# Two-block transformer kernel: choice of experts on VectorE in another order and layout, and products with both parts of x joined into one

## The reference

```python
def squared_relu_mlp(h, w_up, w_down):          # w_up 1024 x 4096, w_down 4096 x 1024
    return jnp.square(jax.nn.relu(h @ w_up)) @ w_down
```

```python
q = (t @ w_q).reshape(T, 8, 2, 128)
s = jnp.einsum('thsd,hskd->thsk', q, sub_keys)          # 2 x 128 scores per head
v_half, i_half = lax.top_k(s, 16)
cand = (v_half[:, :, 0, :, None] + v_half[:, :, 1, None, :]).reshape(T, 8, 256)
best, pos = lax.top_k(cand, 16)
i1 = take_along_axis(i_half[:, :, 0], pos // 16); i2 = take_along_axis(i_half[:, :, 1], pos % 16)
experts, gates = i1 * 128 + i2, softmax(best)
act = gelu(einsum('td,tkd->tk', x, expert_u[experts])) * gates
out = einsum('tk,tkd->td', act, expert_v[experts])
```

## Time and profile before

| | us |
|---|---|
| median of 3 runs (lowest, highest) | 1515.65 (1515.44, 1515.95) |
| the profiled execution | 1515.26 |
| its span | 1513.5 |
| PE busy | 1435.5 (95%) |
| DVE busy | 1060.0 (70%) |
| ACT busy | 757.6 (50%) |
| POOL busy | 70.2 (5%) |

### The profile page before, as it was taken

How to read it: one execution, slowest core, us unless ns; L and a number is a source line. 1 busy time by engine, 2 the same in 40 slices (tenths; PEclk the granted TensorE clock), 3 DMA queues, 4 the chain that set the end, 5 groups by cost and what they waited for, 6 DMA issues and landing times.

```text
span 1513.5 us, 26922 instructions
## 1 busy us (share of the span) xinstructions
PE 1435.5 (95%) x9273; PEld 1293.6 (85%) x9273; DVE 1060.0 (70%) x1981; ACT 757.6 (50%) x1211; POOL 70.2 (5%) x87
## 2 busy tenths in 40 slices
PE   7889889999899997989989999999999999999997
PEld 7867769899798886889979999999999999988886
DVE  6897665555668577569997999555555555567775
ACT  6644654444556533454544555444444444444453
POOL 0200100000000621000000000000000000000000
PEclk9999999999999999999999999999999999999999
DMA  7442325565344522454546888755757566577753
GB/s 280 139 130 96 126 84 188 186 192 183 112 144 161 169 82 70 153 181 154 167 152 185 256 257 259 226 189 184 249 183 245 182 220 210 190 239 249 249 194 140
DMA packets 103208, 274.54 MB, mean 181 GB/s; under 512 B 8160, under 2 KB 41056, under 8 KB 102640
## 3 DMA queue, kind: packets, MB, share of 16 engines
q1 hardware_dynamic: 64832, 237.11, 48.4%
q10 hardware_dynamic: 38032, 34.63, 6.8%
q0 software_dynamic: 288, 2.10, 0.4%
HBM read 254.93 MB, written 18.87 MB: 181 GB/s over the span
## 4 chain that ended last, share of the span: by engine, by line
PE 80%; DVE 15%; ACT 2%; issue 2%; POOL 0%; DMA 0%; POOLq 0%; ACTq 0%; DVEq 0%; SPq 0%
PE Y L1803 43%; PE AO L1803 34%; DVE wl L950 4%; DVE CV L1034 2%; PE M L1803 2%; ACT wh L471 1%; DVE eqs L1558 1%; DVE I L1478 1%; DVE SCO L1494 1%; DVE I L1492 1%; DVE PU L1533 0%; DVE V L1500 0%; DVE V L1486 0%; DVE eqs L1572 0%; DVE xn L973 0%
## 5 line engine op out<-in xcount | busy, mean ns | idle before, releaser
L950 DVE TENSOR_TENSOR wl<-raw,wh 128x1024 fp32r<-128x1024 f32 x440 | 541.6, 1234 | 278.2 <-ACT wh L471 277.4
L471 ACT CAST wh<-raw 128x1024 fp32r<-128x1024 f32 x440 | 460.0, 1048 | 186.7 <-PE AO L1803 92.3
L1803 PE MATMUL AO<-xh,wh 128*128 128x256 f32 (+1 forms) x1776 | 511.0, 288 | 8.6 <-DVE wl L950 7.3
L1803 PE MATMUL AO<-xh,wl 128*128 128x256 f32 (+1 forms) x1776 | 503.4, 283 | 0.0
L1803 PE MATMUL AO<-xl,wh 128*128 128x256 f32 (+1 forms) x1776 | 503.4, 283 | 0.0
L1803 PEld LDWEIGHTS AO<-xh,wh 128*128 128x128 f32 x1776 | 338.5, 191 | 16.3 <-DVE wl L950 9.0
L1803 PEld LDWEIGHTS AO<-xl,wh 128*128 128x128 f32 x1776 | 337.8, 190 | 4.6 <-issue 0.2
L1803 PEld LDWEIGHTS AO<-xh,wl 128*128 128x128 f32 x1776 | 338.7, 191 | 0.0
L1803 PE MATMUL Y<-wh,peer_ah 128*128 128x512 f32 x512 | 200.7, 392 | 2.1 <-DVE peer_al L1620 2.1
L1803 PE MATMUL Y<-wh,peer_al 128*128 128x512 f32 x512 | 200.3, 391 | 0.0
L1803 PE MATMUL Y<-wl,peer_ah 128*128 128x512 f32 x512 | 199.1, 389 | 0.0
(11 more groups left out here) (305 smaller groups left out, 1672.2 us busy)
## 6 DMA issues: line engine op xcount, KB each, us to landing
raw<-in_stream SPq DMA_DIRECT2D x440, 512.0 KB, 3.4
gate_spill<-gstage ACTq DMA_DIRECT2D x32, 512.0 KB, 5.2
gates<-gate_spill ACTq DMA_DIRECT2D x6, 2048.0 KB, 14.9
gates<-gate_spill ACTq DMA_DIRECT2D x8, 512.0 KB, 7.2
rowg<-in_post SPq DMA_DIRECT2D x3, 512.0 KB, 4.4
X<-in_x SPq DMA_DIRECT2D x2, 512.0 KB, 4.8
memx<-in_mem SPq DMA_DIRECT2D x1, 1024.0 KB, 8.1
keys<-in_keys POOLq DMA_DIRECT2D x1, 1024.0 KB, 6.7
```

The lines of the kernel that those rows point to most:

```text
L471: nc.scalar.copy(wh[:, s, :], raw[:, s, :]).then_inc(split_hi, 1)
L950: nc.vector.tensor_tensor(wl[:, s, :], raw[:, s, :], wh[:, s, :].bitcast(F32), ALU.subtract)\
L1803: return nc.tensor.matmul(o, a, b, start=start, stop=stop)
```

## The change

In the MLP and in the paired stage, x's two parts lie side by side in one tile, and the high weights meet both in one matmul of 512 columns that fills a whole bank of AO; the low weights times `xh` go into the first half. The halves are then added: ACT copies the second, DVE adds the first. In the paired stage DVE's sum goes to `up_s` and ACT does the gelu from there, one chunk later.

In the choice of experts the estimates of `turn` are others, the sum keeps its remainder, the layouts put heads innermost, the table of ranks holds each rank 128 times (17 x 128, made by POOL later), PE turns NAT round after chunk 26 (FIRST_TURN), and the last two plain chunks come behind it. ACT's plain chunks 20 to 28 are written out.

```diff
+FIRST_TURN = PLAIN - 2
+SPLIT_EVERY = 1.55
...
-        xh = sb("xh", [P, KT, TM], F32R)
-        xl = sb("xl", [P, KT, TM], F32R)
+        xhl = sb("xhl", [P, KT, 2, TM], F32R)
+        xh, xl = xhl[:, :, 0, :], xhl[:, :, 1, :]
...
ACT, mlp
-                    nc.scalar.activation(hid[:, s, :], AO[:, s, 0:T], func).then_inc(a_free, 1)
+                    nc.scalar.copy(hid[:, s, :], AO[:, s, T:]).then_inc(hid_part, 1)
ACT, plain chunks
+            for c in range(EXP_AT, PLAIN):
+                if c == FIRST_TURN:
+                    act.wait_ge(top_turn, 1)
+                    for j in range(TT):
+                        nc.scalar.copy(picks[:, :, P * j:P * j + P],
+                                       M[:, j, 0:3 * P].rearrange("p (n t) -> p n t", n=3)).then_inc(top_T, 1)
+                hidden(c, P0 + c, c)
+                split(P0 + 4, c)
ACT, both
-                act.wait_ge(hid_lo, c + (FF_CHUNKS + 1))
                 split(P0 + AHEAD + 4 + 2 * s, 0, i)
-                nc.scalar.activation(hid[:, c, :], AO[:, s, 0:T], ACT.Gelu).then_inc(a_free, 1)
+                if not (type(c) is int and c == 0):
+                    act.wait_ge(a_free, c + (A_BASE["peer"] + AHEAD))
+                nc.scalar.copy(up_l[:, s, :], AO[:, s, T:]).then_inc(up_part, 1)
+                if not (type(c) is int and c == 0):
+                    curved(c - 1, 1 - s)
+            def curved(c, s):
+                nc.scalar.activation(hid[:, c, :], up_s[:, s, :], ACT.Gelu).then_inc(curve, 1)
...
+            act.wait_ge(a_free, A_BASE["peer"] + AHEAD + PAIRED)
+            curved(PAIRED - 1, 1)
DVE, mlp (and low now stands ahead of the first split)
+                    dve.wait_ge(hid_part, i * 2 + (base + s + 1))
+                    nc.vector.tensor_tensor(hid[:, s, :], AO[:, s, 0:T], hid[:, s, :], ALU.add).then_inc(a_free, 1)
                     dve.wait_ge(a_free, i * 2 + (free_base + s + 1))
DVE, turn
-                if turns[0] > 1.5 and turns[1] < PLAIN:
+                while turns[0] >= SPLIT_EVERY and turns[1] < FIRST_TURN:
                     split(P0 + 4, turns[1])
-                    turns[0] = 0.0
+                    turns[0] -= SPLIT_EVERY
                     turns[1] += 1
DVE, choice (estimates of max 0.13 to 0.14, index and replace 0.21 to 0.27, shifts 0.2 and 0.33 to 0.29 and 0.45)
-            turn(nc.vector.tensor_copy(I16B[:, :, :, :], I16[:, :, :, :]), 0.6)
+            for j in range(TT):
+                turn(nc.vector.tensor_copy(I16B[:, j, :, :, :].rearrange("p s a h -> p h s a"),
+                                           I16[:, j, :, :].rearrange("p (h s) a -> p h s a", s=2)), 0.35)
...
-                                                 PF[:, half, j, :][:, :, None].to_broadcast([P, HK, TOPK]),
-                                                 ranks[:, half, :][:, None, :].to_broadcast([P, HK, TOPK]),
-                                                 ALU.is_equal), 1.1)
+                                                 PF[:, half, j, :][:, None, :].to_broadcast([P, TOPK, HK]),
+                                                 ranks[:, 1 - half:TOPK + 1 - half, :], ALU.is_equal), 1.25)
...
-                        e, e, IB[:, j, :, half, :][:, :, None, :].to_broadcast([P, PEER_H, TOPK, TOPK]), ALU.mult), 1.1)
+                        e, e, I16B[:, j, half, :, :][:, :, None, :].to_broadcast([P, TOPK, TOPK, PEER_H]), ALU.mult),
+                        1.25)
...
-                        a, b = eqs[:, half, :, 0:n], eqs[:, half, :, n:2 * n]
+                        a, b = eqs[:, half, 0:n, :], eqs[:, half, n:2 * n, :]
-                        turn(nc.vector.tensor_tensor(out_, a, b, ALU.add), n * 0.07)
+                        turn(nc.vector.tensor_tensor(out_, a, b, ALU.add), n * 0.07 + 0.1)
...
             one_hots(0)
+            for c in range(FIRST_TURN, PLAIN):
+                split(P0 + 4, c)
DVE, both
                 split(P0 + AHEAD + 4 + 2 * s, 0, i)
+                summed(c, s)
+            def summed(c, s):
+                dve.wait_ge(up_part, c + 1)
+                if not (type(c) is int and c < 2):
+                    dve.wait_ge(curve, c - 1)
+                nc.vector.tensor_tensor(up_s[:, s, :], AO[:, s, 0:T], up_l[:, s, :], ALU.add).then_inc(a_free, 1)
DVE, ahead of the last stage
+            dve.wait_ge(curve, PAIRED)
POOL, in place of the table at the start
+            nc.gpsimd.iota(ranks[:, :, :], [[1, TOPK + 1], [0, HK]], base=0, channel_multiplier=0,
+                           allow_small_or_imprecise_dtypes=True).then_inc(ranked, 1)
PE, called in mlp (up, and first_pair as first_wide) and in both
+            def pair_products(s, bank, ready=None):
+                o = AO[:, bank, :].rearrange("p (n t) -> p n t", n=2)
+                for kt in range(KT):
+                    if ready:
+                        ready(kt)
+                    h, l = wh[:, s, P * kt:P * kt + P], wl[:, s, P * kt:P * kt + P]
+                    if kt < KT - 1:
+                        mm(o, h, xhl[:, kt, :, 0:T], kt == 0, False)
+                    ins = mm(o[:, 0, :], l, xh[:, kt, 0:T], False, False)
+                    if kt == KT - 1:
+                        ins = mm(o, h, xhl[:, kt, :, 0:T], False, True)
+                return ins
PE, plain chunks
+            for c in range(EXP_AT, FIRST_TURN):
+                pe.wait_ge(a_free, A_BASE["peer"] + c - 1)
+                up(c, P0 + c, c % 2, 0)
             pe.wait_ge(top_nat, TT)
...
             ins.then_inc(top_turn, 1)
+            for c in range(FIRST_TURN, PLAIN):
+                pe.wait_ge(a_free, A_BASE["peer"] + c - 1)
+                up(c, P0 + c, c % 2, 0)
```

More of the change, by code:

```diff
@@ L228, in build @@
         gstage = at("gstage", [P, 2, KEYS, BATCH], 114688)
+        up_l = at("up_l", [P, 2, T], 98304)
+        up_s = at("up_s", [P, 2, T], 100352)
         keys = at("keys", [P, 16, KEYS], 122880)
         SCO = at("SCO", [P, TT, 16, KEYS], 65536)
[L231 removed]
+        eqs = at("eqs", [P, 2, TOPK, HK], 81920, BF16)
         cand = at("cand", [P, TT, PEER_H, CANDS], 90112)
@@ L234, in build @@
         I16 = at("I16", [P, TT, 16, TOPK], 98304, U32)
-        I16B = at("I16B", [P, TT, 16, TOPK], 100352, BF16)
+        I16B = at("I16B", [P, TT, 2, TOPK, PEER_H], 100352, BF16)
         BV = at("BV", [P, TT, PEER_H, TOPK], 101376)
@@ L697, in mlp @@
                         split(b0 + 2 * c + 4, 0)
-            mlp("mlp", FF_CHUNKS, mlp_hid, mlp_act, mlp_ah, ACT.Copy, 0)
+            mlp("mlp", FF_CHUNKS, mlp_hid, mlp_act, mlp_ah, 0)
             tile_high(4, 2)
@@ L829, in hidden @@
                 nc.scalar.activation(hid[:, c, :], AO[:, s % 2, 0:T], ACT.Gelu).then_inc(a_free, 1)
[L831 to L843, removed]
+            with act.Fori(0, EXP_AT // 4) as i:
+                for s in range(4):
+                    hidden(i * 4 + s, P0 + s, s, i)
+                    split(P0 + 4, s, i)
+            act.wait_ge(top_sub, 1)
+            nc.scalar.activation(BV[:, :, :, :], BV[:, :, :, :], ACT.Exp).then_inc(top_exp, 1)
+            for c in range(EXP_AT, PLAIN):
[6 more added lines that the diff above has]
+                split(P0 + 4, c)
             def gates_out(c, s):
@@ L1206, in mlp @@
                     hidden(s, s, 0)
+                    low(s, 0)
                     split(up_block(b0, s) + 4, 0)
-                    low(s, 0)
                     if s:
@@ L1213, in mlp @@
                         hidden(i * 2 + s, s, i)
+                        low(s, i)
                         split(b0 - 1 + 2 * s + 4, 0, i)
-                        low(s, i)
                         split(b0 - 1 + 2 * s + 5, 0, i)
@@ L1569, in _ @@
                     for half in range(2):
[L1570 to L1572 removed]
+                        a, b = eqs[:, half, 0:n, :], eqs[:, half, n:2 * n, :]
+                        out_ = NAT[:, j, half, :][:, None, :] if n == 1 else a
+                        turn(nc.vector.tensor_tensor(out_, a, b, ALU.add), n * 0.07 + 0.1)
             dve.wait_ge(top_exp, 1)
[L1574 removed]
+            turn(nc.vector.tensor_reduce(gsum[:, 0, :], BVV, AX_X, ALU.add), 0.4)
             step.wait()
[L1576 removed]
+            turn(nc.vector.reciprocal(gsum[:, 1, :], gsum[:, 0, :]), 0.25)
             step.wait()
             for j in range(TT):
[L1579 to L1582 removed]
+                nc.vector.tensor_tensor(NAT[:, j, 2, :].rearrange("p (k h) -> p k h", h=PEER_H),
+                                        BV[:, j, :, :].rearrange("p h k -> p k h"),
+                                        gsum[:, 1, PEER_H * j:PEER_H * j + PEER_H][:, None, :]
+                                        .to_broadcast([P, TOPK, PEER_H]), ALU.mult).then_inc(top_nat, 1)
+            while turns[1] < FIRST_TURN:
                 split(P0 + 4, turns[1])
@@ L2068, in up @@
                     pe.wait_ge(a_free, i * 2 + (A_BASE[name] + s - 1))
-                    wide_products(b % SLOTS, bank, xh, xl, T).then_inc(w_used, 1)
```

(3 more changed lines are left out.)

57 lines of the change are left out of this document (28 added, 29 removed).

## The result

The changed kernel takes 1497.43 us (median of four runs, 1496.89 to 1499.77), the kernel before 1515.55 beside it: 0.9885 of it (95% interval 0.9869 to 0.9900), 18 us faster. Forecast were 1503.4, in a range from 1497.5 to 1508.0. The direction is right, the size is one third too small. The profiled execution has a span of 1496.1, against 1513.5.

A forecast was written before the change was run, and what follows sets the result against it. PE held 80% of the chain of waits, DVE 15%. From the median 1515.65, choice -10.2, paired stage -2.9, MLP 0 and hand-over +0.9 sum to -12.2, giving 1503.4 us; range 1497.5 to 1508.

The forecast's parts named there:

- The choice: Choice of experts: PE loses less to DVE's work there, 10.2 us gained; bounds from 11.2 down to 5.9.
- The comparisons: Choice of experts: four comparisons with the rank table fall from 2285 to 1218 ns each, 4.3 us less; bounds 0 and 4.3.
- the halvings: Choice of experts: the sums' last two halvings fall from 424 and 413 to 289 ns, 1.0 us less.
- I16B 0.2: Choice of experts: one cast becomes two half-size turned casts, 0.2 us added, PF's 0.1; bounds for both 0 and 0.9.
- The wait for NAT: Choice of experts: PE stands at the transposes at 791.5 and waits 1.0 us until NAT is ready at 792.5.
- The pairs in the paired stage: Paired stage: each merged product saves 5.6 ns, times 8 times 64, 2.9 us less; bounds 0 and 4.9.
- The MLP: MLP: merging estimated between 0.4 us more and 1.4 less, taken as 0; period 5.60 as before.
- The hand-over: Before the last stage: the last sum and gelu, with two signals, come uncovered before low of chunk 64, 0.9 us more.
- The second one: All merged stages: a fixed time saved for every removed product, in the MLP too, 1499.0; chance 0.12.
- the first: MLP and paired stage: columns alone count, so the pairs give PE nothing, 1506.3; chance 0.20.
- the third: Choice of experts gives less: the comparison stays at 2285 ns, NAT 2.1 to 4.3 us later, 1505.5 to 1507.7; chance 0.08.
- The fourth: Paired stage: ACT and DVE wait for each other across the sum, delaying PE in each of 64 chunks, 1537.4; chance 0.05.

The follow-up runs named there:

- e12_far: The changed kernel, 512-column products kept, but x's two parts as far apart as in the kernel before: 1494.16 us, ratio 0.9874.
- e9_pad: The kernel before with 512 unused bytes per partition between the buffers of x's high and low parts: 1515.41 us, ratio 1.0000.
- e6_dense: The changed kernel with gates added to the experts' activations instead of multiplied, making the down products' operand dense: 1497.54 us, ratio 0.9890.
- e0_before: The kernel before, unchanged, traced on another chip: 1515.63 us, ratio 1.0001.
- e3_unmerged: The changed kernel, layout kept, with seven of eight 512-column products per up block split into fourteen of 256 columns: 1504.73 us, ratio 0.9929.
- e4_cover: The changed kernel with ACT's and DVE's work for chunk 64 put ahead of chunk 63's sum, before the last stage: 1494.45 us, ratio 0.9863.
- e5_late_turn: The changed kernel with PE turning the rank table after all 28 plain chunks instead of after 26: 1500.68 us, ratio 0.9908.
- e2_pairs: The kernel before with only the merged 512-column products and side-by-side x of the MLP and paired stage: 1506.01 us, ratio 0.9943.
- e7_layout: The kernel before with only x's two parts side by side in one buffer, every product unchanged: 1509.34 us, ratio 0.9957.
- e1_choice: The kernel before with only the edits of the choice of experts: 1502.99 us, ratio 0.9914.

## Why the prediction was right, and where it was not

- *The choice, -10.2 forecast, -10.45 measured.* The sum is right by two errors that cancel. The comparisons (1222 against 1218), the halvings (286 and 288 against 289) and the two chunks that cover the one-hots came as reckoned. The term "I16B 0.2" was mis-sized: two turned casts stand in the chain with 1.34 us where one of 0.43 stood, 0.9 more, and with PF's 0.23 that is past the upper bound given for both, 0.9. With it the first wait is 1.70 instead of 1.2. The wait for NAT is 1.3 instead of 1.0. By positions, chunk 0 to the first one-hot product is 86.5 us long against 85.2 forecast, so 8.9 us are gained, not 10.2. (The first one-hot product stands at 799.5, earlier than the 801.7 forecast, only because chunk 0 starts 3.5 us earlier.) The other 1.55 come from a thing that the prediction left out: in the kernel before the 16 products behind the stall of 2.6 us ran at half clock and took 3.50 us, now 1.95 from the start of the first. That the stage's sum is right is luck.
- *The pairs in the paired stage, -2.9 forecast, -5.9 measured* ((5.607 - 5.513) x 63). This is the step that was mis-sized: "2 x 118.3 - 231 = 5.6 ns" took the neighbouring 512-column products as a fixed measure. The up block came out at 2.79 as forecast, but the down block, whose instructions nobody touched, went from 2.76 to 2.72. e12_far shows a merged product saving 10 ns with the down block left alone; near buffers move some of the saving from the up to the down block, by a mechanism that stays open. e9_pad (address), e6_dense (data) and e0_before (chip) rule three out. The upper bound of 4.9 was too low.
- *The MLP, 0 forecast.* The period is 5.60 in steady state as forecast, for a reason not seen: merging gives 1.7 us (e3_unmerged, e12_far), the near layout costs as much. Of the 1.0 us gained 0.7 is the wait for mlp_al at the end, 0.2 instead of 0.9.
- *The hand-over, +0.9 forecast, +1.0 measured,* and 1.55 behind it at half clock, which the prediction did not have. e4_cover takes both away.
- *Stretches without an edit, 0 forecast, -2.6 measured.* Up to 1.4 of it is the clock between 570 and 615; the rest is not settled.
- *The rivals.* The second one named the mechanism that the runs show (each removed product saves a fixed time, in the MLP too) and its 1499.0 was nearest. Columns alone do not count, so the first is out; the third is out with the comparison's 1222 ns. The fourth, a chain across the sum, did not come: no wait for low in the steady paired stage. The Trainium skill, "TensorE: Matmul & The Clock Gate", section "Back-to-back issue gap", has a fixed cost of 2.5 ns for an isolated product, an estimated 1.9 us for the 768. In this kernel's stream it is 7 to 10 ns: 512 x 10 + 256 x 7 = 6.9 us with the buffers as they were, and 10 and 8 ns with the near ones (e3_unmerged).

Put together, measured less forecast: paired -3.0, the hand-over +0.1, the half clock behind it +1.55, the choice -0.25, the MLP -1.0, from there to the choice -1.7, the first stage -0.8, the gates -0.1. That is the -5.2 between -12.2 and -17.4. The range held by luck in part: its lower edge was the second rival with 1.5 us added for what was costed at nothing, and of the -5.2, 2.6 come from stretches that nobody edited.

## What to carry to other kernels

When PE runs its products back to back without waiting, fewer and wider ones gain a fixed time each (7 to 10 ns here), but measure the layout that makes the wide operand possible by itself: it can give or take as much. A wait of PE of about 2 us (1.8 to 2.7 here) cost 1.5 to 3.4 us more in the products behind it in some of these kernels and nothing in others, so price it as a range, wait alone to wait plus half clock, and cover it even if it looks small. Do not add up partial edits by their total times when unedited stretches move by 1 to 4 us: read each edit in its own stage.

## What the runs showed of the hardware

- Two traces of the kernel before (the first and e0_before) have the stretches at half clock at the same places from 160 us on, and at different ones ahead of that; a kernel that differs in an unrelated later stage can have them at other places (from 480 to 500 us 0.91 in the changed kernel and 1.00 in e5_late_turn). After the wait of 2.5 us for the one-hots they came in the kernel before and in e5_late_turn and stayed away in e2_pairs and e7_layout; after the wait of 1.8 to 1.9 us before the last stage they came in the changed kernel and e6_dense (0.55 both), e5_late_turn (0.65) and e3_unmerged (0.68), and in e2_pairs and e12_far the same wait was followed by 3.6 us at 1.00. No half clock followed the wait of 0.9 us there. An isolated one costs 1.5 to 1.8 us.
- Two buffers read in turn by neighbouring products: side by side instead of 8.7 KB apart they make unmerged products of the paired stage 0.5% faster and those of the MLP 0.6% slower, in one trace, where the MLP also moved by 0.4% in e1_choice without an edit; merged, 0.3% faster and 1.0% slower. 512 bytes more between them do nothing.
- A cast from 32-bit integers to bf16 into a turned layout takes 868 ns for 256 elements a partition, where 512 in order take 430.
